# Half of the tokens of a product-key expert layer computed densely instead of gathered

## The chip, the cores and the metric

The program runs on one core of a Trainium2 chip. The metric is the device time of one execution in microseconds (us); the number given is the median of several runs. All data are f32.

## The reference, cut to what matters

Two transformer-like blocks follow each other on 512 tokens of width 1024. The change touches only the last part of the second block, a layer that picks 16 experts for each of 8 heads and each token, out of 128 x 128 = 16384 experts, each with one row u and one row v of 1024 numbers:

```python
q = (xb @ w_query).reshape(TOKEN_BLOCK, P_HEADS, 2, P_HALF)
s = jnp.einsum('thpk,hpnk->thpn', q, sub_keys)
sv, si = lax.top_k(s, P_TOPK)
cand = (sv[:, :, 0, :, None] + sv[:, :, 1, None, :]).reshape(TOKEN_BLOCK, P_HEADS, 256)
cidx = (si[:, :, 0, :, None] * N_KEYS + si[:, :, 1, None, :]).reshape(TOKEN_BLOCK, P_HEADS, 256)
fv, fpos = lax.top_k(cand, P_TOPK)
eidx = jnp.take_along_axis(cidx, fpos, axis=-1)
g = jax.nn.softmax(fv, axis=-1)
act = jax.nn.gelu(jnp.einsum('td,thkd->thk', xb, u_tab[eidx]))
out = jnp.einsum('thk,thkd->td', g * act, v_tab[eidx])
```

A residual sum and a final norm over each token follow.

## The kernel before

Each engine runs its own hand-written list of instructions, and semaphores order them. The 512 tokens are T = 4 tiles of 128, a token per partition in this stage. Weights stream through a ring of two 2 MB buffers (`ring`), loaded by the SP queue. The first layers take up to about 1355 us and stay as they are.

The expert stage begins with 32 projection chunks (`QUERIES`): each multiplies eight 128x128 weight tiles with 256 tokens (`chunk_pe`, L562), ScalarE copies the result (L1655), and `sub_scores` (L1416) multiplies it with the sub-keys. For each tile and head VectorE then runs a picking job in four pieces: `pick_keys` (top 16 of 128 scores, twice), `pick_pairs` (top 16 of the 256 sums), `pick_experts` (the expert numbers by comparing with `iota`), `pick_gates` (the softmax weights, with ScalarE's exponentials). There are 4 x 8 = 32 jobs.

A "pick" is one slot of one tile: NPICK = 512 of them, 128 per tile. For pick n GpSimd issues an indirect DMA (L2040) that fetches one row of `peer_uv` for each of the 128 tokens, u and v side by side, 8 KB per token, 1 MB in all, into a row buffer (`rows`, 10 to 14 slots in turn). VectorE makes the dot product with the token (`dot`, L1948), ScalarE the GELU and the weight (`weights`, L1630 and L1631), and then the row v is added with that weight, either on VectorE (`value`, L1960) or on TensorE: ScalarE writes a diagonal matrix of the weights (L1637), and TensorE multiplies it with v into two PSUM banks (`values`, L1468). `on_pe` sends about five of eight picks to TensorE. A row slot is free for the next gather when its value is done. VectorE runs picks in order, and puts one piece of a later job after every fourth pick; `lag_of` lets values trail the dot products by up to three picks. At the end of each tile five steps (`last`, L1969 to L1986) add the residual, norm and store.

## Time and profile before

| | us |
|---|---|
| median of 3 runs | 2700.69 |
| lowest, highest | 2699.71, 2701.6 |
| span of the profiled execution | 2699.1 |
| busy: TensorE (PE) | 2168.8 |
| busy: VectorE (DVE) | 1675.7 |
| busy: ScalarE (ACT) | 794.1 |
| busy: GpSimd (POOL) | 626.4 |

All profile numbers come from one execution. A view of groups gives, for a line of the program, an engine and an operation, the count, the busy time, the mean time of one in ns, and the idle time just before them with what ended it. A view of stretches gives the same busy times for a window of the span, with the clock that TensorE was granted (1.00 is 2.4 GHz) and the share of the 16 DMA engines that was busy. One f32 product of TensorE shows as two records, each with its own weight load (PEld); the 256 products of the query stage are 512 records. Durations of neighbouring records can overlap, so the distance of their starts is what a repeated operation costs.

### The profile page before, as it was taken

How to read it: one execution, taken by the hardware profiler on the slowest of the kernel's cores; microseconds unless marked ns; L12 is line 12 of the kernel's file. 1: busy time of each engine (PE TensorE's matmuls, PEld its weight loads, DVE VectorE, ACT ScalarE, POOL GpSimd, SP SyncE). 2: the span in 40 equal slices, each digit the busy share in tenths (PEclk: the TensorE clock that was granted, in tenths of full speed). 3: DMA queues.
4: the chain of work that ended last, by engine and by line, in shares of the span. 5: the costliest groups of instructions: out<-in, count | busy, mean ns of one | idle time of the engine just before them, and what ended most of it. 6: DMA issues, size and time to landing. Idle time of an engine off the chain costs nothing.

```text
span 2699.1 us, 20390 instructions
## 1 busy us (share of the span) xinstructions
PE 2168.8 (80%) x6274; PEld 1025.0 (38%) x6274; DVE 1675.7 (62%) x3651; ACT 794.1 (29%) x2184; POOL 626.4 (23%) x543
## 2 busy tenths in 40 slices
PE   6999999999999999999989666656565665556665
PEld 3454555444444444454478222223222222222221
DVE  5444454220114505234679888889889988889876
ACT  2022364110000002222333334334333334334332
POOL 0000000000000000000024444444444444444442
PEclk9999999999999999999999777888877788888778
DMA  9621010211236511211169999999999999999996
GB/s 371 241 102 63 32 63 32 80 76 62 89 129 258 210 62 65 76 47 63 47 236 370 407 427 427 427 427 427 427 427 427 427 426 425 428 425 420 421 423 275
DMA packets 85545, 692.66 MB, mean 257 GB/s; under 512 B 9504, under 2 KB 9504, under 8 KB 10688
## 3 DMA queue, kind: packets, MB, share of 16 engines
q0 software_dynamic: 77520, 590.33, 52.7%
q1 hardware_dynamic: 7200, 96.47, 9.4%
q10 hardware_dynamic: 720, 4.62, 0.4%
q8 instruction: 47, 0.77, 0.1%
q14 instruction: 58, 0.48, 0.0%
HBM read 689.28 MB, written 2.10 MB: 256 GB/s over the span
## 4 chain that ended last, share of the span: by engine, by line
PE 48%; DMA 29%; DVE 16%; issue 5%; POOL 1%; ACT 1%; POOLq 0%; DVEq 0%; ACTq 0%
PE PS L562 22%; DMA arena<-in_peer_uv,arena 20%; PE PS L592 8%; DMA ring<-in_peer_uv,arena 8%; DVE arena L1960 4%; PE PS L1104 4%; PE PS L1150 3%; DVE arena L1948 3%; PE PS L747 2%; PE PS L1468 2%; DVE ring L1948 1%; PE PS L767 1%; PE PS L756 1%; DMA arena<-in_ada 1%; PE PS L1125 1%
## 5 line engine op out<-in xcount | busy, mean ns | idle before, releaser
L1468 PE MATMUL PS<-arena 128*128 128x512 f32 x768 | 476.8, 771 | 320.1 <-ACT arena L1637 300.3
L2040 POOL DMA_INDIRECT arena<-in_peer_uv,arena x340 | 410.0, 1206 | 925.9 <-DVE arena L1930 461.5
L1948 DVE CUSTOM_DVE_ANT_0 arena<-arena 128x1024 f32<-128x1024 f32 x340 | 414.0, 1226 | 101.0 <-DMA arena<-in_peer_uv,arena 98.4
L1468 PEld LDWEIGHTS PS<-arena 128*128 128x128 f32 x768 | 177.1, 244 | 604.0 <-ACT arena L1637 415.7
L1468 PE MATMUL PS<-ring,arena 128*128 128x512 f32 x428 | 259.4, 755 | 138.9 <-ACT arena L1637 130.2
L562 PE MATMUL PS<-arena,ring 128*128 128x512 f32 x832 | 359.2, 593 | 2.1 <-issue 0.8
L1630 ACT ACTIVATE arena<-arena 128x1 f32<-128x1 f32 x512 | 103.2, 202 | 776.3 <-DVE arena L1948 775.5
L562 PE MATMUL PS<-hT,ring 128*128 128x256 f32 (+1 forms) x928 | 301.5, 486 | 7.0 <-ACT arena L1655 4.2
L2040 POOL DMA_INDIRECT ring<-in_peer_uv,arena x172 | 201.6, 1172 | 214.5 <-DVE arena L1960 159.4
L1948 DVE CUSTOM_DVE_ANT_0 ring<-ring,arena 128x1024 f32<-128x1024 f32 x172 | 209.1, 1226 | 45.2 <-DMA ring<-in_peer_uv,arena 42.8
L562 PEld LDWEIGHTS PS<-arena,ring 128*128 128x128 f32 x832 | 157.0, 190 | 203.2 <-issue 201.9
L562 PEld LDWEIGHTS PS<-hT,ring 128*128 128x128 f32 x928 | 179.9, 195 | 123.7 <-issue 99.9
L592 PE MATMUL PS<-hT,ring 128*128 128x512 f32 x512 | 222.1, 597 | 1.7 <-ACT hT L382 1.7
L2026 POOL DMA_DIRECT2D arena<-in_ada x20 | 10.7, 538 | 899.2 <-ACTq L343 668.5
L1468 PEld LDWEIGHTS PS<-ring,arena 128*128 128x128 f32 x428 | 101.0, 247 | 294.8 <-ACT arena L1637 183.2
L1960 DVE SCALAR_TENSOR_TENSOR arena<-arena 128x1024 f32<-128x1024 f32 x145 | 185.7, 1281 | 0.1
L1631 ACT ACTIVATE arena<-arena 128x1 f32<-128x1 f32 x512 | 150.8, 294 | 16.6
L592 PEld LDWEIGHTS PS<-hT,ring 128*128 128x128 f32 x512 | 98.0, 192 | 125.3 <-issue 124.2
L1780 DVE TENSOR_SCALAR arena<-PS 128x512 f32<-128x512 f32 x32 | 22.1, 691 | 196.0 <-PE PS L592 196.0
L1766 DVE SCALAR_TENSOR_TENSOR xT<-PS,modc,xT 128x512 f32<-128x512 f32 x24 | 18.0, 751 | 179.9 <-PE PS L562 179.9
L1637 ACT ACTIVATE arena<-cst,arena 128x128 f32<-128x128 f32 x299 | 120.1, 402 | 9.8
L1104 PE MATMUL PS<-hT,ring 128*128 128x512 f32 x256 | 117.9, 604 | 0.0
(321 smaller groups left out, 2231.4 us busy)
## 6 DMA issues: line engine op xcount, KB each, us to landing
ring<-in_wstream SPq DMA_DIRECT2D x45, 2048.0 KB, 7.5
arena<-in_ada POOLq DMA_DIRECT2D x24, 2048.0 KB, 8.7
arena<-in_peer_uv,arena POOLq DMA_INDIRECT x340, 17.6
ring<-in_peer_uv,arena POOLq DMA_INDIRECT x172, 17.6
xT<-in_xT POOLq DMA_DIRECT2D x1, 2048.0 KB, 18.5
arena<-in_alibi ACTq DMA_DIRECT2D x1, 2048.0 KB, 14.4
result<-arena SPq DMA_DIRECT2D x3, 512.0 KB, 7.7
arena<-in_subkeys ACTq DMA_DIRECT2D x1, 1024.0 KB, 4.8
```

The source lines that it names most:

```text
L562: ins = pe.matmul(o, l, r, start=(a == 0), stop=(a == len(lhs) - 1))
L592: ins = pe.matmul(bank(j % 2, n), w[:, k, m * P:(m + 1) * P], act_in(k), start=(k == 0), stop=(k == kc - 1))
L747: ins = pe.matmul(o, l, r, start=True, stop=True)
L1104: ins = pe.matmul(bank(7), w[:, k, tile(j % 4)], hT[:, k, :], start=(k == 0), stop=(k == KD - 1))
L1150: ins = pe.matmul(bank(5 + j % 2), lhs, rhs, start=(k == 0), stop=(k == KD - 1))
L1468: ins = pe.matmul(bank(6 + b), diag[:, k % NDIAG, :], rows[slot_of(n)][:, D + b * 512:D + (b + 1) * 512], start=opens, stop=closes)
L1630: own(act.activation(dots[:, e:e + 1], dots[:, e:e + 1], ACT.Gelu))
L1631: act.activation(wexp[:, t, e:e + 1], dots[:, e:e + 1], ACT.Copy, scale=gate[:, t, e:e + 1]).then_inc(wexp_ok, 1)
L1637: act.activation(diag[:, k % NDIAG, :], ident, ACT.Copy, scale=wexp[:, t, e:e + 1]).then_inc(diag_ok, 1)
L1948: dve.tensor_tensor_reduce(u, u, h2tok[t % 2], 1.0, 0.0, ALU.mult, ALU.add, dots[:, e:e + 1]).then_inc(dot_ok, 1)
L1960: dve.scalar_tensor_tensor(out=a, in0=v, scalar=wexp[:, t, e:e + 1], in1=a, op0=ALU.mult, op1=ALU.add)\
L2040: pool.indirect_dma_start(rows[j], None, ap["peer_uv"], bass.IndirectOffsetOnAxis(ap=eidx[:, t, e:e + 1], axis=0)).then_inc(landed[j], 16)
```

## The change

Tiles 0 and 1 (256 tokens) keep the gathers: NPICK is 256. For tiles 2 and 3 no row is gathered. Every expert is computed for all 256 tokens, and a table of gates, zero where an expert was not picked, selects:

- The experts are 128 chunks of 128; chunk j holds the experts i x 128 + j. `dense_dots(j)` multiplies u of the chunk (a new input `u_turned`, laid out for it, 0.5 MB per chunk) with the 256 tokens, eight products of 256 columns. `dense_gelu(m)` applies GELU to two chunks, `dense_weights(m)` multiplies them with the gates, and in the last loop TensorE multiplies the weights with v of the chunk (rows of `peer_uv` at a distance of 128 rows, 4 KB of each), four products of 512 columns, summed in PSUM over all chunks.
- The gate tables are a product of one-hot matrices: for each token, the first one-hots (128 picks x first key, times the gate) and the second ones (128 picks x second key). VectorE makes both: `first_one_hots` in 256 TENSOR_SCALARs of 128x128, `second_one_hots` in 32 TENSOR_TENSORs of 128x1024. TensorE multiplies them (`gate_tables`, 64 groups of four 128x128 products), ScalarE copies the result, and 16 blocks of 1 MB go to DRAM and are read back in another order, in pieces of 512 bytes, while the chunks run. A path that makes first one-hots on ScalarE exists in the code; `made_on_dve` returns True for all groups.
- The order: 24 "beats" first. Beats 0 to 15 hold one job of tile 2 or 3 and two picks each, beats 16 to 23 three picks; four beats also hold a job of tile 0. Beats 8 to 23 each make four groups of gate tables. The 56 picks of the beats have their values on TensorE, and dots and GELU of 24 chunks (AHEAD) run in beats 7 to 14. Queries alternate between the halves of the tokens, each pair of queries followed by its scores for two tiles, and ScalarE and TensorE put four queries to a beat.
- Then the last loop: TensorE runs chunks c = 0 to 127, each with the dots of chunk c + 24 and the values of chunk c. The 200 other picks run beside it, all with values on VectorE. `pick_at` ties a chunk to 1.73 picks.
- Row slots: 3 up to pick 13, 6 up to 35, then 7. The SP queue loads u (three buffers), v (three), and gates (two).
- The last steps of tiles 1, 2 and 3 follow each other after everything else.

```diff
+NGT = 2
+NPICK = NGT * NSLOT
 NDIAG = 4
+NCHUNK = 128
+AHEAD = 24
+NBEAT = 24
 BLK = 4096
...
+def made_on_dve(g):
+    return True
...
+def dense_pair(b, q):
+    m = 3 * (b - 7) // 2 + q
+    return m + 1 if 7 <= b < 15 and m < 3 * (b - 6) // 2 else 0
+def pick_at(chunk):
+    return NEARLY + (max(0, chunk) * 173) // 100
...
+            for j in range(AHEAD + 3):
+                if j == 0:
+                    sp.wait_ge(mm_done, MM0["pq"] + 1)
+                if j >= 3:
+                    sp.wait_ge(s_done, j - 2)
+                sp.dma_start(ubuf[j % 3], ap["u_turned"][j]).then_inc(u_loaded[j % 3], 16)
+            def load_values(j):
+                sp.dma_start(vbuf[j % 3], value_rows[j]).then_inc(vt_loaded[j % 3], 16)
+            def load_gates(blk):
+                sp.dma_start(gstage[blk % 2].rearrange("p (a c) -> p a c", a=16),
+                             gates_in_dram[:, :, blk * P:(blk + 1) * P].rearrange("a p c -> p a c")).then_inc(g_loaded[blk % 2], 16)
+            sp.wait_ge(g_pe, 64)
+            load_values(0)
+            for q in range(2):
+                sp.wait_ge(g_stored[q], 16 * 8)
+            load_gates(0)
+            load_values(1)
+            load_gates(1)
+            load_values(2)
+            for c in range(NCHUNK):
+                if c + AHEAD + 3 < NCHUNK:
+                    sp.wait_ge(s_done, c + AHEAD + 1)
+                    sp.dma_start(ubuf[c % 3], ap["u_turned"][c + AHEAD + 3]).then_inc(u_loaded[c % 3], 16)
+                if c + 3 < NCHUNK:
+                    sp.wait_ge(d_done, c + 1)
+                    load_values(c + 3)
+                if c % 8 == 0 and c // 8 + 2 < 16:
+                    sp.wait_ge(w_ok, 4 * (c // 8 + 1))
+                    load_gates(c // 8 + 2)
+                if c == 80:
+                    sp.wait_ge(fin_ok, 1)
+                    sp.dma_start(out[0:P, :], acc[0]).then_inc(stored, 16)
...
+            def dense_dots(j):
+                pe.wait_ge(u_loaded[j % 3], 16 * (j // 3 + 1))
+                if j % 2 == 0 and j >= 4:
+                    pe.wait_ge(s_ev, j // 2 - 1)
+                for k in range(KD):
+                    ins = pe.matmul(dense_bank(j), ubuf[j % 3][:, tile(k)], hT[:, k, 256:512], start=(k == 0), stop=(k == KD - 1))
+                ins.then_inc(s_done, 1)
+            def turn_picks(td):
+                pe.wait_ge(picks_ok, td + 1)
+                pe.wait_ge(pk_ev, 16)
+                if td == 1:
+                    pe.wait_ge(picks_ev, 1)
+                for q in range(2):
+                    pe.transpose(PS[:, 3, tile(q)], selij[:, td, q, :], ident)
+                pe.transpose(PS[:, 3, tile(2)], gate[:, 2 + td, :], ident).then_inc(picks_pe, 1)
+            def gate_tables(g):
+                if made_on_dve(g):
+                    pe.wait_ge(a_dve, MADE_DVE[g + 1])
+                else:
+                    pe.wait_ge(a_act, MADE_ACT[g + 1])
+                pe.wait_ge(b_ok, g // 2 + 1)
+                if g >= 2:
+                    pe.wait_ge(g_ev, g - 1)
+                for q in range(4):
+                    ins = pe.matmul(PS[:, 4 + g % 2, tile(q)], aone[:, g % 2, q, :], bone[:, (g // 2) % 2, 4 * (g % 2) + q, :],
+                                    start=True, stop=True)
+                ins.then_inc(g_pe, 1)
+            for b in range(6, NBEAT):
+                values(beat_picks(b - 1))
+                if b >= 7:
+                    for q in range(4):
+                        if q < 2 and dense_pair(b, q):
+                            dense_dots(2 * dense_pair(b, q) - 2)
+                            dense_dots(2 * dense_pair(b, q) - 1)
+                        if b in (8, 16) and q == 0:
+                            turn_picks(b // 8 - 1)
+                        if b >= 8:
+                            gate_tables(4 * (b - 8) + q)
+            values(beat_picks(NBEAT - 1))
+            pe.wait_ge(picks_ev, 2)
+            pe.wait_ge(g_ev, 64)
+            for c in range(NCHUNK):
+                if c + AHEAD < NCHUNK:
+                    dense_dots(c + AHEAD)
+                pe.wait_ge(w_ok, c // 2 + 1)
+                pe.wait_ge(vt_loaded[c % 3], 16 * (c // 3 + 1))
+                for td in range(2):
                     for half in range(2):
-                        ins = turn(hT, t + 1, half, half)
-                    ins.then_inc(tt_pe, 1)
-                    values(t * NSLOT + 36, t * NSLOT + 44)
-                    pe.wait_ge(tt_ev, 3 + t)
-                for half in range(2):
-                    ins = turn(xT, t, half, half)
-                ins.then_inc(x_turned, 1)
-                values(t * NSLOT + (44 if t + 1 < T else 36), t * NSLOT + 48)
-                if 0 < t < T - 1:
-                    scores_of(t + 1)
-                values(t * NSLOT + 48, n1)
+                        ins = pe.matmul(bank(2 + 2 * td + half), weights_of(c)[:, tile(td)], vbuf[c % 3][:, half * 512:half * 512 + 512],
+                                        start=(c == 0), stop=(c == NCHUNK - 1))
+                ins.then_inc(d_done, 1)
...
+            def dense_gelu(m):
+                act.wait_ge(s_done, 2 * m + 2)
+                if m == 8:
+                    act.wait_ge(pk_keys, JOB[2, PH - 1] + 1)
+                if 2 * m >= AHEAD:
+                    act.wait_ge(d_done, 2 * m + 2 - AHEAD)
+                act.activation(weight_pair(m), bank(m % 2).rearrange("p (c n) -> p c n", c=2), ACT.Gelu).then_inc(s_ev, 1)
...
+            def second_one_hots(m):
+                if m % 16 == 0:
+                    dve.wait_ge(picks_ev, m // 16 + 1)
+                if m >= 2:
+                    dve.wait_ge(g_pe, 2 * m - 2)
+                c = 8 * (m % 16)
+                dve.tensor_tensor(bone[:, m % 2, :, :], const("iota").unsqueeze(1).to_broadcast([P, 8, P]),
+                                  pick_j[:, c:c + 8].unsqueeze(2).to_broadcast([P, 8, P]), ALU.is_equal).then_inc(b_ok, 1)
+            def first_one_hots(g):
+                if g >= 2:
+                    dve.wait_ge(g_pe, g - 1)
+                for q in range(4):
+                    c = 4 * (g % 32) + q
+                    ins = dve.tensor_scalar(aone[:, g % 2, q, :], const("iota"), pick_i[:, c:c + 1], pick_g[:, c:c + 1],
+                                            ALU.is_equal, ALU.mult)
+                ins.then_inc(a_dve, 1)
+            def dense_weights(m):
+                blk = m // 4
+                dve.wait_ge(s_ev, m + 1)
+                dve.wait_ge(g_loaded[blk % 2], 16 * (blk // 2 + 1))
+                w = weight_pair(m).rearrange("p c (a t) -> p c a t", a=16)
+                g = gstage[blk % 2].rearrange("p (a c t) -> p c a t", a=16, t=16)[:, 2 * (m % 4):2 * (m % 4) + 2, :, :]
+                dve.tensor_tensor(w, w, g, ALU.mult).then_inc(w_ok, 1)
...
+            job(0)
+            gated = 0
+            for b in range(NBEAT):
+                if b < 16:
+                    k = JOB[2 + b // 8, b % 8]
+                    job(k, gated)
+                    gated = k
+                picks = beat_picks(b)
+                dot(picks[0])
+                if b in (16, 19, 23):
+                    pick_gates(gated)
+                for n in picks[1:]:
+                    dot(n)
+                if b in GATHER_JOB_AT:
+                    hd = GATHER_JOB_AT[b]
+                    k = JOB[hd // PH, hd % PH]
+                    if b < 16:
+                        job(k, gated)
+                    else:
+                        job(k)
+                    gated = k
+                if b >= 8:
+                    for q in range(4):
+                        g = 4 * (b - 8) + q
+                        if q % 2 == 0:
+                            second_one_hots(g // 2)
+                        if made_on_dve(g):
+                            first_one_hots(g)
+            done, m = NEARLY, 0
+            for n in range(NEARLY, NPICK):
                 dot(n)
                 while done < min(n + 1 - lag_of(n), NPICK):
-                    if not on_pe(done):
-                        value(done)
+                    value(done)
                     done += 1
-                if n in (1, 3, 5):
-                    pick(1, (n + 1) // 2)
-                if n % 4 == 1 and n // PK + 2 < NHEAD:
-                    pick(n // PK + 2, n % PK // 4)
-                t, e = n // NSLOT, n % NSLOT
-                if t > 0 and e in LAST_AT:
-                    last(t - 1, LAST_AT.index(e))
+                while m < NCHUNK // 2 and n >= max(NEARLY + 2 + m, pick_at(2 * m + 1 - 14)):
+                    dense_weights(m)
+                    m += 1
+                for back, piece in ((13, pick_keys), (11, pick_pairs), (9, pick_experts), (5, pick_gates)):
+                    hd = (n + back) // PK
+                    if (n + back) % PK == 0 and 5 <= hd < NGT * PH:
+                        piece(JOB[hd // PH, hd % PH])
+                if n >= NSLOT and n - NSLOT in LAST_AT:
+                    last(0, LAST_AT.index(n - NSLOT))
```

## Rows read from the trace of the kernel before

**Rows 1.** The page: busy tenths in 40 slices, granted clock, DMA share, GB/s.

```profile
PE   6999999999999999999989666656565665556665
...
DVE  5444454220114505234679888889889988889876
...
PEclk9999999999999999999999777888877788888778
DMA  9621010211236511211169999999999999999996
GB/s 371 241 102 63 32 63 32 80 76 62 89 129 258 210 62 65 76 47 63 47 236 370 407 427 427 427 427 427 427 427 427 427 426 425 428 425 420 421 423 275
```

**Rows 2.** Stretches: length, busy us of each engine (records), granted clock, DMA share, GB/s.

```profile
600.00:700.00 100.00, 100.00 (x234) 44.27 (x233) 9.67 (x14) 9.46 (x15) 0.00 (x0) 1.00 0.23 84
1000.00:1100.00 100.00, 97.07 (x281) 43.49 (x280) 38.33 (x62) 20.32 (x32) 0.00 (x0) 0.98 0.17 63
...
1450.00:1500.00 50.00, 42.54 (x207) 35.31 (x207) 47.58 (x89) 17.55 (x56) 24.68 (x18) 0.95 0.94 355
1500.00:1600.00 100.00, 64.19 (x116) 24.91 (x114) 87.76 (x187) 36.44 (x112) 49.04 (x42) 0.79 1.01 425
1600.00:1800.00 200.00, 121.14 (x200) 46.92 (x200) 176.13 (x378) 75.69 (x232) 94.87 (x81) 0.80 1.01 427
```

**Rows 3.** Timeline at the start of the query stage: start us, us, engine, line, operation.

```profile
1355.80 10.19 PE L562 MATMUL PS<-hT,ring 128*128 128x256 f32 x32 [1.72 <-ACT hT L382]
...
1366.56 0.68 PE L1416 MATMUL PS<-arena 128*128 128x128 f32 x4 [0.56 <-ACT arena L1655]
...
1367.69 0.49 DVE L1890 MAX8 arena<-arena 128x8 f32<-128x128 f32 x2 [8.18 <-ACT arena L1660]
...
1373.23 0.17 DVE L1920 TENSOR_SCALAR arena<-arena 128x16 uint32<-128x16 uint32 x1
1373.31 0.17 DVE L1921 TENSOR_SCALAR arena<-arena 128x16 uint32<-128x16 uint32 x1
...
1376.04 10.53 PE L562 MATMUL PS<-hT,ring 128*128 128x256 f32 x48
1376.19 0.17 DVE L1930 CAST arena<-arena 128x16 uint32<-128x16 f32 x1
...
1376.64 0.99 POOL L2040 DMA_INDIRECT arena<-in_peer_uv,arena  x1 [461.51 <-DVE arena L1930]
```

**Rows 4.** DMA queues from 1600 to 1800 us: packets, MB, share of 16 engines.

```profile
q0 software_dynamic: 11706, 85.28, 101.0%
```

**Rows 5.** DMA queues and issues in the last 9.1 us of the span.

```profile
q1 hardware_dynamic: 288, 0.52, 14.9%
...
result<-arena SPq DMA_DIRECT2D x2, 256.0 KB, 2.0
```

**Rows 6.** The gathers' line L2040: time from issue to landing.

```profile
DMA to landing us min/median/max: 5.6/17.6/23.1
```

**Rows 7.** Groups from 1340 us on, by form: busy, mean ns, idle before them.

```profile
L1948 DVE CUSTOM_DVE_ANT_0 arena<-arena 128x1024 f32<-128x1024 f32 x340 | 414.0, 1226 | 101.0 <-DMA arena<-in_peer_uv,arena 98.4 <-DVE arena L1902 0.4
...
L1960 DVE SCALAR_TENSOR_TENSOR arena<-arena 128x1024 f32<-128x1024 f32 x145 | 185.7, 1281 | 0.1
...
L1924 DVE TENSOR_TENSOR arena<-arena,cst 128x512 f32<-128x512 f32 x32 | 22.1, 692 | 1.1
...
L1972 DVE TENSOR_TENSOR arena<-arena,sq 128x1024 f32<-128x1024 f32 x4 | 4.9, 1219 | 0.0
```

**Rows 8.** Groups before 1350 us, by form: a TENSOR_SCALAR with two scalars.

```profile
L818 DVE TENSOR_SCALAR arena<-arena,smalls 128x128 f32<-128x128 f32 x16 | 5.5, 346 | 0.6
```

**Rows 9.** Timeline of the end: start us, us, engine, line, operation.

```profile
2685.79 1.23 DVE L1948 CUSTOM_DVE_ANT_0 arena<-arena 128x1024 f32<-128x1024 f32 x1 [1.21 <-DMA arena<-in_peer_uv,arena]
...
2689.64 1.22 DVE L1969 TENSOR_TENSOR arena<-arena,PS 128x1024 f32<-128x1024 f32 x1
...
2695.30 1.42 DVE L1986 SCALAR_TENSOR_TENSOR arena<-arena,smalls 128x512 f32<-128x512 f32 x2
```

614 lines of the change are left out of this document (371 added, 243 removed).

## The prediction

> **What bounds the kernel now.** I read the page's slices first [rows 1]. Up to about slice 20 TensorE is nine tenths busy at full clock; from there to the end the DMA engines are full, at 427 GB/s, and TensorE is down to five or six tenths at a granted clock of 0.7 to 0.8. So there are two stages with two limits. The table of stretches says the same with numbers [rows 2]: from 1500 us on TensorE is busy 64% or less and its clock is 0.79 to 0.80 of 2.4 GHz, the DMA share is 1.01, VectorE is busy 88%. The change touches only what follows 1356 us, where the last projection (the queries) starts [rows 3]; everything ahead of it is the same program.
>
> The tail is 512 gathers of 128 x 8 KB, 1.0486 MB each. At 427 GB/s one takes 2.456 us, and 512 take 1257 us. The first starts at 1376.6 [rows 3], the last dot product at 2685.8 [rows 9]: 1309 us. So 96% of that stretch is the gathers, and the row of the DMA engines shows that hardly anything else is moving [rows 4]. VectorE has 2.51 us of work on a pick that it handles wholly (1.226 + 1.281 us, [rows 7]), so it is close behind.
>
> **The change part by part.** It removes 256 gathers, half of the stage: 629 us of DMA time. In their place stand, for the other 256 tokens, all 128 blocks of 128 experts: the loads of u (128 x 0.524 MB in 4 KB rows), of v (as much), gate tables written once (16 x 1.049 MB) and read once (the same bytes in 512 B pieces), dense products on TensorE, and one-hot matrices that VectorE makes. By bytes that is 168 MB, 393 us at 427 GB/s. The DMA bill alone falls by 236 us. What spoils this is that the work now comes in two phases, one after the other: the beats (jobs, one-hots, gate tables) and the main loop (values).
>
> Terms that I use. A 512-column f32 product is two records of 0.427 us (234 records fill 100 us at clock 1.00, [rows 2]), so 0.854 us; a 256-column one is two of 0.219 us (48 in 10.53 us, [rows 3]), so 3.50 us for the 8 of a query or of a dense dot; four 128-column ones are 8 records, some 1.05 us (4 in 0.68 us, [rows 3]; down to 0.13 each). A picking job on VectorE, without waits, is 1367.69 to 1376.36 [rows 3], 8.7 us with its last conversion; with the gate step 9.1. A gather lands 5.6 us after its issue at the least [rows 6], and the issue takes about 1 us.
>
> *Queries and beats 0 to 7.* The first picking job now waits for a third query, 1372 in place of 1367.7. TensorE has 30 queries after the first two (105 us), 15 score groups (16 us), transposes (3), and values of 10 picks (17, each 1.71): from 1367 to 1508. Picks share three row slots in this part, so a slot passes from TensorE's value to the next gather, dot product and weight; that loop is about 19.6 us per beat, which is also what TensorE has to do in it. Picks 14 and 15 go to slots in the weight ring, which are free after the last query; with pick 13's slot freed at 1512 they land at 1519 or so. Job (2,7) follows: beat 8 starts at about 1532.
>
> *Beats 8 to 15.* VectorE has a job (9.1), two dot products (2.35) and four groups of one-hots. The first one-hots are 16 TENSOR_SCALARs of 128x128 with two operands of a scalar kind; the nearest row is 346 ns, and two in a row overlap by some 0.08 us, so 0.26 each [rows 8]. The bounds are 0.35 (no overlap) and 0.17 (half hidden, as with the 0.17 us steps of the first job that start 0.08 apart, [rows 3]); the second ones are two of 128x1024 at 1.22 [rows 7]. A group is 1.06 + 0.61. TensorE has 3.4 of values, 4.3 of gate tables and one or two dense pairs of 7.0. In the beats with two pairs (four of them) the second pair stands between two gate tables and VectorE must wait for it, because it has two buffers only: 23.9 us; in the others 18.2. With the extra job in beat 11 and the copying of the picks: 1532 + 17 + 96 + 64 + 13 = 1722 at the first table of beat 16.
>
> *Beats 16 to 23.* VectorE has 3.5 + 6.7 = 10.2 us per beat, TensorE 9.4, DMA 3 gathers and one table, 9.8: three about equal. Seven beats, two jobs (17.4) and the last groups: 94 us. The phase ends at about 1816, say 1810, as the dense jobs leave out two small steps. So 434 us pass from the first gather with only 213 us of DMA work in them. If the one-hots cost 0.17 us each this is 23 us shorter, at 0.35 it is 23 us longer.
>
> *Main loop.* It starts with a hole: the first gates must come back from DRAM, VectorE waits for them with the weights of pick 57 behind it, and ScalarE waits for two finished chunks at pick 57. 22 us pass before gathers run freely (7 picks are in slots by then). Then DMA has to do 193 gathers (474 us), 99 loads of u and 125 of v, 14 of gates, and 2.5 us of small ones. A 4 KB row: between a packet of 2 KB, 0.085 us (14.9% of 16 engines in 9.1 us is 21.7 us, for 256 of them, [rows 5]), and one of 8 KB in the full stretch (2.456 us for 8 per engine, 0.307); on that line it is 0.159, and 8 of them per engine are 1.27 us. u 126, v 159. A 512 B piece on the same line is 0.028 us, 128 per engine are 3.6 us, 14 loads 50 us; the low end is the bytes at 427 GB/s, 34 us, the high end a 2 KB packet's 0.085 us, 152 us. I take 50, the line's. Sum 812 us.
>
> TensorE in the same loop: 104 chunks of 3.50 + 3.42 and 24 of 3.42 are 802 us, at clock 1.00, from about 13 us after the start. That is the same as DMA, within 2%. VectorE: 200 picks of 2.51 (502), 11 jobs (100), 64 weight products of 0.69 (44), and 5: 651 us, not the bound. Two equal loads with buffers of three chunks lose a little to each other; I estimate 1%, 8 us, and count to 30 in the range.
>
> *End.* After the last row lands: dot 1.2, weight 1.5, two values 2.5, then twelve steps of the last three tiles at 1.22 (15, [rows 9] for the like), roots 1.5, store 2.5: 24 us, against 12 now.
>
> Sum: 1810 + 22 + 812 + 8 + 24 = 2676 us of span. The span now is 2699.1 and the median 2700.7, 1.6 more, so **2678 us**, 0.8% less. Nearly all of the 236 us of DMA time that is saved is given back while the DMA engines stand half idle in the beats.
>
> At one place a rule of the Trainium skill speaks against this. The rows of v for one chunk are i x 128 + j of a table of 8 KB rows: 4 KB pieces, 1 MiB apart from partition to partition. No row of this trace has such a pitch, the gathers being scattered and the weight blocks contiguous. "DMA: Bandwidth & Descriptors", section "Latency and other measured facts", gives copies at a pitch of 512 KiB 207 GB/s and at 2 MiB 164, where the full rate is 214. By the page the 159 us of v would be an estimate of 164 to 207.
>
> **Rivals.**
> *Slow pieces (slower).* The small or far-apart pieces of the gates and of v cost more than the line through 2 KB and 8 KB. Place: the main loop, DMA-bound. It decides from 17 us of extra on (2678 to 2695); a third more on v alone (53) gives 2731, all of the gates' high end (102) gives 2780. For it: none of these shapes is in the trace. Against: even the 2 KB packets run at 24 GB/s per engine, the same as large ones.
> *The clock (slower).* TensorE's clock was 1.00 and 0.98 at 100% and 97% busy, 0.95 at 85%, 0.79 at 64% [rows 2]. If waits for chunks keep it at a mean of 0.9 of 2.4 GHz, between these rows, its 802 become 891 us: 1810 + 13 + 891 + 17 + 1.6 = 2733. It decides below a mean of about 0.94. Against: a TensorE that is the bound is always busy, and then the clock comes back.
> *The beats are shorter (faster).* The one-hots are pipelined at 0.17 us and the pair between two tables costs VectorE nothing: 23 + 24 us off, and 2631. For it: small operations of the first job start 0.08 us apart. Against: the pair is TensorE's work in any case.
> That the change doesn't do what it says I leave out: half of the gathers go away whatever the rest does.
>
> **Chances.** Forecast 0.49 (2650 to 2706; six sevenths of it below 2695), shorter beats 0.16, slow pieces 0.22, the clock 0.13. A measurement of this kernel can tell 0.2% from no change, 5.4 us. Faster: 0.16 + 0.42 = 0.58; within 0.2% 0.07 (all of it from the forecast case); slower 0.35. The range is 2610 to 2765: it leaves out a tenth at each side.
>
> **What would show it.** Right: 256 gathers; DMA share near one half from 1380 to 1800 and near 1.0 afterwards; granted clock above 0.95 in the main loop; the last gate table's product at 1780 to 1840; TENSOR_SCALAR of 128x128 near 0.35 us with a start every 0.26. Wrong: a DMA share of 1.0 at much less than 427 GB/s in the main loop (slow pieces); TensorE always busy at a clock of 0.8 or 0.9; or VectorE or ScalarE waiting for each other in the main loop with both DMA and TensorE idle, which I hold at a few us only. The largest doubt is where the beats end; each us there is a us of the result.

## The result and the profile after

The changed kernel takes 2776.0 us (median of 4 runs, 2763.54 to 2777.31) against 2700.2 of the kernel before: ratio 1.0271, 95% interval 1.0250 to 1.0292. The prediction was 2678, 22 us faster; it came out 76 us slower, outside the range. The span of the profiled execution is 2775.0 us, the forecast of it was 2676.

The page after: slices for TensorE, granted clock, DMA and GB/s, then the two large queues (packets, MB, share of 16 engines).

```profile
PE   6999999999999999998998877668999999989877
...
PEclk9999999999999999999999999889999999999989
DMA  9621021112156411110244656779999999999995
GB/s 368 236 92 61 31 71 51 61 61 91 60 227 227 151 61 61 67 55 31 94 172 148 242 187 229 306 265 354 405 387 388 388 389 400 395 400 379 369 370 208
...
q0 software_dynamic: 40656, 321.93, 29.4%
q1 hardware_dynamic: 76944, 247.48, 24.4%
```

The shape is the forecast one: the DMA engines are half empty up to about slice 27 and full from slice 28 on. TensorE is nine tenths busy in most slices, with six to eight tenths in slices 22 to 28 (beats 8 to 23 and the start of the loop). What differs from [rows 1] is that the full DMA engines move 369 to 405 GB/s (slices 29 to 39) and not 427. By stretch (length, busy us of each engine, granted clock, DMA share, GB/s), with the main loop's 700 us as one:

```profile
1548.00:1725.00 177.00, 140.02 (x663) 111.59 (x664) 142.62 (x476) 77.37 (x130) 16.42 (x17) 0.92 0.57 202
1725.00:1830.00 105.00, 74.26 (x329) 50.32 (x328) 89.50 (x249) 54.77 (x104) 25.26 (x22) 0.85 0.71 276
...
1900.00:2600.00 700.00, 659.77 (x2224) 435.65 (x2223) 491.95 (x893) 124.80 (x407) 189.60 (x157) 0.96 0.99 387
```

The main loop is the counterpart of [rows 2]: both DMA (share 0.99) and TensorE (660 of 700 us) are nearly full, the clock is 0.96, and VectorE is idle for 30% of the time. It is idle because it waits, not because it has time to spare (below).

I split the 99 us between the forecast span and the real one at three marks. The last gate table's product starts at 1827.5 instead of 1810: 18. The first dense value starts at 1850.6, 23 us later; the hole of 22 is as forecast. The last dot product of a gather starts at 2725.8, so the loop took 876 us from 1850 where I had 812 + 8: 56. From there to the end are 49 us, not 24: 25. So: beats 18, loop 56, tail 25. The end of the kernel after, VectorE (start, us):

```profile
2725.82 1.22 DVE L2182 CUSTOM_DVE_ANT_0 arena<-arena 128x1024 f32<-128x1024 f32 x1
...
2761.40 1.22 DVE L2242 TENSOR_TENSOR arena<-PS,sq 128x1024 f32<-128x1024 f32 x1 [24.65 <-PE PS L1628]
```

In [rows 9] the last steps follow the last dot at once. Here VectorE waits 24.65 us for TensorE, which still has dense chunks to do.

What comes from memory in the main loop, by the page's DMA issues (count, KB each, us to landing): the gate tables, read in 512 B pieces, take 22.7 us to land, while 1 MB stored contiguously, when the DMA engines are half empty, takes 5.8.

```profile
arena<-in_u_turned SPq DMA_DIRECT2D x128, 512.0 KB, 9.0
arena<-in_peer_uv SPq DMA_DIRECT2D x128, 512.0 KB, 9.2
...
gate_tables<-arena ACTq DMA_DIRECT2D x16, 1024.0 KB, 5.8
arena<-gate_tables SPq DMA_DIRECT2D x16, 1024.0 KB, 22.7
```

### The profile page after: what moved, and what is told of

Same layout as the page of the kernel before. It is cut to its first block, busy times and chain, and to the rows that moved or that the text cites. A ratio compares the mean times of both kernels' runs of the same rounds, so it can differ in the third digit from the quotient of the medians.

```text
span 2775.0 us, 24927 instructions
## 1 busy us (share of the span) xinstructions
PE 2532.4 (91%) x8876; PEld 1459.4 (53%) x8876; DVE 1487.6 (54%) x3441; ACT 652.0 (23%) x1559; POOL 314.1 (11%) x287
## 4 chain that ended last, share of the span: by engine, by line
PE 73%; DMA 14%; DVE 10%; issue 1%; ACT 1%; SPq 1%; POOL 0%; DVEq 0%; ACTq 0%; POOLq 0%
PE PS L609 24%; PE PS L1579 12%; PE PS L1628 11%; DMA arena<-in_u_turned 9%; PE PS L639 8%; PE PS L1151 4%; PE PS L1197 3%; PE PS L794 2%; DMA arena<-in_peer_uv 1%; PE PS L1602 1%; PE PS L814 1%; PE PS L803 1%; DMA arena<-in_ada 1%; DVE arena L2221 1%; PE PS L1172 1%
## 5 line engine op out<-in xcount | busy, mean ns | idle before, releaser
L1579 PE MATMUL PS<-hT,arena 128*128 128x256 f32 x2048 | 488.4, 395 | 60.4 <-DMA arena<-in_u_turned 60.4
L1579 PEld LDWEIGHTS PS<-hT,arena 128*128 128x128 f32 x2048 | 406.5, 199 | 171.6 <-DMA arena<-in_u_turned 71.1
L609 PE MATMUL PS<-arena,ring 128*128 128x512 f32 x832 | 359.2, 593 | 2.1 <-issue 0.8
L2342 POOL DMA_INDIRECT arena<-in_peer_uv,arena x151 | 176.2, 1167 | 1158.3 <-DVE arena L2153 465.7
L2182 DVE CUSTOM_DVE_ANT_0 arena<-arena 128x1024 f32<-128x1024 f32 x151 | 183.9, 1222 | 97.5 <-DMA arena<-in_peer_uv,arena 95.5
L1628 PE MATMUL PS<-arena,hT 128*128 128x512 f32 x384 | 173.6, 598 | 14.1 <-DVE hT L2231 14.1
L1628 PE MATMUL PS<-arena,ring 128*128 128x512 f32 x320 | 146.6, 603 | 15.3 <-DMA arena<-in_peer_uv 15.2
L2182 DVE CUSTOM_DVE_ANT_0 ring<-ring,arena 128x1024 f32<-128x1024 f32 x105 | 127.9, 1223 | 38.8 <-DMA ring<-in_peer_uv,arena 37.3
L1628 PE MATMUL PS<-arena 128*128 128x512 f32 x320 | 143.9, 593 | 1.6 <-DMA arena<-in_peer_uv 1.4
L1602 PE MATMUL PS<-arena 128*128 128x128 f32 x512 | 78.7, 315 | 72.3 <-DVE arena L2221 68.9
L1602 PEld LDWEIGHTS PS<-arena 128*128 128x128 f32 x512 | 73.1, 223 | 83.8 <-DVE arena L2221 78.2
## 6 DMA issues: line engine op xcount, KB each, us to landing
arena<-gate_tables SPq DMA_DIRECT2D x16, 1024.0 KB, 22.7
```

The source lines that it names most:

```text
L609: ins = pe.matmul(o, l, r, start=(a == 0), stop=(a == len(lhs) - 1))
L1579: ins = pe.matmul(dense_bank(j), ubuf[j % 3][:, tile(k)], hT[:, k, 256:512], start=(k == 0), stop=(k == KD - 1))
L1602: ins = pe.matmul(PS[:, 4 + g % 2, tile(q)], aone[:, g % 2, q, :], bone[:, (g // 2) % 2, 4 * (g % 2) + q, :], start=True, stop=True)
L1628: ins = pe.matmul(bank(2 + 2 * td + half), weights_of(c)[:, tile(td)], vbuf[c % 3][:, half * 512:half * 512 + 512], start=(c == 0), stop=( ...
L2182: dve.tensor_tensor_reduce(u, u, h2tok[t], 1.0, 0.0, ALU.mult, ALU.add, dots[:, e:e + 1]).then_inc(dot_ok, 1)
L2342: pool.indirect_dma_start(rows[j], None, ap["peer_uv"], bass.IndirectOffsetOnAxis(ap=eidx[:, t, e:e + 1], axis=0)).then_inc(landed[j], 16)
```

## The experiments

Theories at the start. A: SyncE's queue is blocked while the gate load's 2048 pieces are taken in, so u and v come late and TensorE stalls. B: the 1 MiB pitch of v costs. C: the total of the gate loads on a full DMA is the price. D: the end of the beats passes on one to one. E came later: in the early beats VectorE's idle time is a wait inside a chain. The recorded expectations of single runs use some letters otherwise: their B is "only the packets' own time counts", and the D of gates_once is "only the held-up queue counts". The kernel before, taken again beside each group of runs, had medians of 2699.9 to 2701.7 us, so times of different groups can be compared.

**The queue after a gate load.** SyncE's queue in the kernel after (start, us, line):

```profile
2102.57 0.33 SPq L1313 DMA_DIRECT2D arena<-in_peer_uv  x1
2102.94 0.43 SPq L1316 DMA_DIRECT2D arena<-gate_tables  x1
2106.02 15.88 SPq L1330 DMA_DIRECT2D arena<-in_u_turned  x1
```

The load of u behind a gate load takes 15.88 us to issue instead of 0.33. TensorE, same stretch:

```profile
2119.60 3.60 PE L1628 MATMUL PS<-arena,ring 128*128 128x512 f32 x8
2128.47 6.67 PE L1579 MATMUL PS<-hT,arena 128*128 128x256 f32 x16 [5.27 <-DMA arena<-in_u_turned]
```

The dots come 5.27 us late and then run at half speed, 6.67 us instead of 3.62. TensorE had been idle before them, and the granted clock of their stretch is 0.54: nearly all of it at the lower level, 1.2 GHz. In the loop TensorE waits 12 times for u, 60.4 us in all. VectorE and GpSimd in the same stretch, then two rows by stretch (the last three numbers are granted clock, DMA share and GB/s):

```profile
2127.24 0.69 DVE L2231 TENSOR_TENSOR hT<-hT,arena 128x512 f32<-128x512 f32 x1 [10.16 <-DMA arena<-gate_tables]
...
2130.54 0.94 POOL L2342 DMA_INDIRECT arena<-in_peer_uv,arena  x1 [12.25 <-DVE arena L2199]
...
2128.50:2135.00 6.50, 6.50 (x17) 5.25 (x18) 6.29 (x16) 0.96 (x4) 0.94 (x1) 0.54 1.02 384
2135.00:2140.00 5.00, 5.00 (x17) 2.91 (x16) 4.86 (x11) 3.41 (x7) 2.61 (x2) 1.00 0.73 228
```

VectorE stands 10.16 us in front of `dense_weights`, which needs this gate load. The dots and values behind it in its list wait too, so no row slot comes free, and GpSimd issues no gather for 12.25 us. A little later the DMA engines run out of work: their share from 2135 to 2140 us is 0.73. Over the loop VectorE waits 154.2 us for gate tables, 14 times. The DMA queues in the 19 us behind the gate load, 2103 to 2122 (q0 the gathers, q1 SyncE's queue with gates, u and v):

```profile
q0 software_dynamic: 761, 5.46, 70.1%
q1 hardware_dynamic: 2107, 2.13, 34.1%
...
arena<-in_u_turned SPq DMA_DIRECT2D x1, 512.0 KB, 22.4
```

The engines are full. But SyncE's queue gets 34.1% of their time, where it has 41.2% on the loop's average (below), the gathers 70.1% where they have 57.5%, and u lands after 22.4 us instead of 9. So the gathers run ahead while what VectorE and TensorE wait for is held up. The Trainium skill's "DMA: Bandwidth & Descriptors", section "Queues, rings and completion order", says that each DMA engine takes turns between the queues, a packet at a time (a packet there is a group of descriptors). If so, a turn of SyncE's queue filled with 512 B pieces is a short one against a turn of 8 KB rows. These rows (34.1% against 70.1%) agree with that; no run isolates it.

### gates_whole: the gate tables read contiguously

```
-  sp.dma_start(gstage[blk % 2].rearrange("p (a c) -> p a c", a=16),
-               gates_in_dram[:, :, blk * P:(blk + 1) * P].rearrange("a p c -> p a c"))
+  sp.dma_start(gstage[blk % 2], gates_in_dram[blk])
```

> This kernel reads each 1 MB block of gate tables back as 128 rows of 8 KB in place of 2048 pieces of 512 bytes; the bytes are the same, but the gates are those of other experts, so its output is not the reference's. Theory A (the SP queue is held up: the load that follows a gate load takes 4 to 19 us to issue, so u arrives late and TensorE stops 2 to 12 us at each of the 14 blocks, some 70 us with the start): the long issues of the SP queue and TensorE's waits for u_turned (60 us) go away, and the time falls by 50 to 80 us, to 2695 to 2725. Theory B (the DMA engines are full and only packets count): 2048 packets of 0.0305 us become 128 of 0.33, 14 blocks x 1.3 us = 18 us less, about 2757.

The chunks get the gates of other experts in this run. Measured: 2716.36 us (2711.68 to 2725.08), ratio 1.0056 (1.0035 to 1.0076). 60 us go with the pieces, the bytes unchanged. (Its profiled execution is the slowest of the four; between the profiled spans it is 52 us.) Its SyncE queue and its main loop:

```profile
1979.62 0.43 SPq L1316 DMA_DIRECT2D arena<-gate_tables  x1
1982.70 0.33 SPq L1329 DMA_DIRECT2D arena<-in_u_turned  x1
```

```profile
1900.00:2600.00 700.00, 678.08 (x2335) 446.02 (x2334) 523.71 (x957) 130.47 (x430) 195.88 (x165) 0.99 1.01 411
```

No long issue, 411 GB/s, the clock 0.99. A gate load lands after 15.4 us instead of 22.7, and VectorE's waits for gate tables fall from 154.2 us to 78.5.

### gates_once: 14 of the 16 gate loads left out

The loads of the tables of blocks 2 to 15 are left out and `dense_weights` uses what is there.

> Leaves out the loads of gate blocks 2 to 15; the weights of all chunks are made with blocks 0 and 1, so the output is not the reference's. The loads took 14 x 128 pieces of 0.0305 us per engine, 55 us of DMA time in the loop. Theory C (the loop is DMA-bound throughout, and the 512 B pieces also hold u and v back behind them, since a piece gets its turn between 8 KB packets of the gathers): the 1 MB blocks as whole rows still cost 2.5 us each, so this is 35 us below the kernel that reads them whole (2716): 2675 to 2690. Theory D (only the held-up queue counts, and TensorE is the bound once it is gone): as with whole rows, 2705 to 2720.

Measured: 2680.7 us (2680.1 to 2683.62), ratio 0.9931 (0.9911 to 0.9950). The last dot moves from 2725.8 to 2636: 90 us of loop, for which my sum had 50. Its slices, its main loop, and the whole loop of this run and of the kernel after:

```profile
GB/s 375 237 109 64 32 64 32 72 86 63 75 140 255 219 63 63 63 63 63 46 112 149 221 190 196 249 305 258 416 417 416 416 414 415 404 412 417 415 403 219
```

```profile
1900.00:2600.00 700.00, 696.67 (x2390) 450.12 (x2388) 547.10 (x978) 134.84 (x451) 213.38 (x176) 1.00 1.01 413
...
1848.00:2636.00 788.00, 780.83 (x2638) 496.27 (x2639) 607.45 (x1068) 145.87 (x496) 232.22 (x193) 1.00 1.00 407
...
1850.00:2726.00 876.00, 798.16 (x2622) 513.07 (x2623) 606.51 (x1068) 149.81 (x496) 232.53 (x193) 0.95 0.98 381
```

Against gates_whole that is 36 us for 14 contiguous loads, 2.5 us each, their bytes at full rate and no more. So pieces of 512 B cost 60 us more than the same bytes in long ones. Their own packets explain only a part: a piece has a mean duration of 0.0305 us in the trace's packet records, 128 per engine and load are 3.9 us, 14 loads 55; the whole ones 35. That is 20 of the 60. The other 40 are in what shares the engines and the buffers with them.

The packet records divide the loop itself. From the first dense value to the last dot it takes 875 us in the kernel after and 788 in gates_once. The packets' own times in it, summed and divided by 16 engines, are 857 and 790 (records of neighbouring packets overlap a little, so full engines come out at slightly more than the time). Of the 88 us, 54 are the pieces themselves. 13 are other packets that take longer beside them: 8 KB ones 0.324 us instead of 0.318, 4 KB ones 0.166 instead of 0.163. The remaining 21 are time in which the engines had too little to do. In gates_once VectorE waits for no gate table in the loop, and TensorE hardly for u. So neither A nor C alone explains the loads: most of the price is on the full DMA engines (C), the rest in engines that wait (A, and VectorE, which A didn't name).

The second fact of this run: even without the pieces the full rate is at most 417 GB/s, not the 427 of [rows 1].

### gates_in_four: the same pieces in four loads

Each gate load in four parts of 512 pieces, behind four successive chunks.

> Each gate block is loaded in four parts of 512 pieces, one after the v load of each of the chunks 8k to 8k+3, instead of all behind chunk 8k. Pieces and bytes are unchanged. Theory A (SP queue held up by one long transfer): no issue is held for more than about 5 us, which the three buffers of u and v cover; TensorE's waits for u fall from 60 us to under 15, and the time to 2705 to 2735. Theory B (the DMA engines are full): no change, 2770 to 2780.

Measured: 2784.47 us (2776.56 to 2789.49), ratio 1.0320 (1.0299 to 1.0341). No gain, and outside what both theories expected; issues of 2 to 12 us still stand behind many of the parts, and TensorE waits 61.4 us for u, where theory A expected under 15. So the long issues are not a matter of one long load. But the edit does a second thing: the last part of a gate load leaves three chunks later, and VectorE's waits for gate tables grow from 154.2 to 202.4 us. The run doesn't separate the two.

### v_whole: v read contiguously

```
-  sp.dma_start(vbuf[j % 3], value_rows[j])
+  sp.dma_start(vbuf[j % 3], ap["u_turned"][j])
```

> The v loads read the contiguous u blocks in place of rows 1 MiB apart, so its output is not the reference's. The rival of slow far-apart rows: packets of 4 KB (0.171 us on average, 0.159 in the median) fall to 0.159 and the time by 10 to 20 us or more. Theory A: the pitch costs nothing, 2770 to 2780, as TensorE's waits are for u and not for v.

Measured: 2774.56 us (2768.82 to 2778.38), ratio 1.0277 (1.0252 to 1.0302), the same as the kernel after. A 4 KB packet has a mean of 0.166 us in the loop, here as in the kernel after. Theory B falls: the pitch costs nothing.

### stored_in_pieces: the pieces moved to the stores

Loads as in gates_whole; the transposition of blocks is made by the stores, in the beats, where the DMA engines have time. The whole result is computed.

```
-  act.dma_start(gates_in_dram[tg], gstage[tg % 2])
+  act.dma_start(gates_in_dram[:, :, tg * P:(tg + 1) * P].rearrange("k p c -> p k c"),
+                gstage[tg % 2].rearrange("p (k c) -> p k c", k=16))
```

> The 512 B pieces move from the loads of the last loop to the 16 stores in beats 8 to 23, where the DMA engines are 30 to 40% idle; the result stays complete. Theory C: the last loop is that of the whole rows (2716), and the stores, 10 us or more apart, hide their pieces; the first gate load lands earlier too, so the start hole of 23 us shrinks by up to 10: 2705 to 2720. If stores in pieces are slow (over 10 us each) and ScalarE waits for the buffer, the beats get longer: 2725 to 2760.

Measured: 2723.76 us (2718.77 to 2726.67), ratio 1.0086 (1.0063 to 1.0109). 52 us back, 4 short of the expected range; the last product of a gate table starts about a us later (1828.7), and ScalarE waits 9.4 us for stores.

### half_values: is TensorE the bound of the loop?

Half of the dense value products (one of the two tiles of dense tokens) are left out, 218 us of TensorE.

> Leaves out half of the dense value products (those of the fourth tile), 256 products of 512 columns, 218 us of TensorE's 802 us in the last loop; all loads, gates and picks stay. Theory C (the loop is bound by the DMA engines): the last dot product stays near 2726 and only the end shortens, by about half of TensorE's 36 us behind it: 2750 to 2765. The rival that TensorE is the bound: 100 to 200 us less. With less to do TensorE's clock may fall; that changes nothing for C.

Measured: 2750.39 us (2748.45 to 2754.3), ratio 1.0194 (1.0176 to 1.0213). Of 218 us, 26 come back: the last dot is at 2714.8, 11 earlier, and the tail 34 us in place of 49. TensorE's granted clock in this loop is 0.88, lower than the 0.95 of the kernel after, and the loop is still shorter. So TensorE doesn't bind the loop. By these rows the DMA engines (share 0.99) do, with VectorE's waits for gate tables, 159 us here, beside them; the time in which the DMA engines had too little to do falls from 18 us to 8.

### slope160 and stored_slope: the tail

The planner's spread of chunks over picks at 1.60 instead of 1.73; stored_slope has it on top of stored_in_pieces.

> One number: the last loop ties a chunk to 1.60 picks in place of 1.73. Theory (the end): the picks end 48 us before the kernel does, because TensorE has some 13 chunks of 3.4 us left by then; ScalarE lets picks run ahead to the edge that pick_at sets. With 1.60 TensorE is 7 chunks further at the same pick, so the tail shrinks by about 20 us. As the DMA time is unchanged, the last dot product comes some 5 us later: 2755 to 2765. If the tail is not set by this edge, no change.

> Both edits: stores in pieces, and 1.60 picks per chunk. If the two are independent, 2716 less 15 to 20: about 2697, the time of the kernel before.

Measured: slope160 2756.75 us (2755.23 to 2759.57), ratio 1.0207 (1.0187 to 1.0226); the last dot is 7.5 us later (2733.3), the wait for TensorE is gone and the tail is 24. stored_slope 2721.78 us (2718.51 to 2723.45), ratio 1.0075 (1.0055 to 1.0095): only 2 us better than stored_in_pieces, since the last dot goes from 2678.6 to 2697. I had added the two gains; with TensorE 697 of 700 us busy and DMA at 1.01 in the loop of stored_slope (1900 to 2600), the work that leaves the tail has no room ahead of it.

### half_on_act and pair_last: the length of the beats

half_on_act makes every second group of first one-hots on ScalarE. pair_last puts the second dense pair of a beat behind the fourth gate table, on TensorE and on ScalarE.

> Every second group of first one-hots is made on ScalarE (eight ACTIVATEs of 128x128, some 0.4 us each, 3.2 us per group) in place of VectorE (1.1 us per group). If VectorE is the bound of beats 8 to 23, at most 32 x 1.1 = 35 us go and the last gate table comes at about 1800 in place of 1828. If ScalarE, which also copies a gate table in 1.05 us and has the weights of the picks, becomes late in its place (2 x 3.2 + 4 x 1.05 + 3 = 14 us per beat against 10 to 11 now), the beats 16 to 23 get longer by 3 us each and the time rises by about 10 to 30 us. I hold the second for likelier: 2785 to 2805.

> In beats 8, 10, 12 and 14 the second dense pair comes behind the fourth gate table instead of between the first and the second. My sum had 23.9 us for such a beat against 18.2, because VectorE waits for the pair. If that wait is the price, the last gate table comes 9 us (TensorE's own 21.7 us per beat then bound) to 23 us earlier than 1828, and the time falls by as much, to 2752 to 2766. If VectorE's 28 us of waits were covered otherwise, no change.

Measured: half_on_act 2835.27 us (2831.47 to 2837.97), ratio 1.0497 (1.0476 to 1.0519), 30 us above the expected range: the last gate table moves by 58.7 us and the time by 59. pair_last 2759.29 us (2752.95 to 2765.0), ratio 1.0232 (1.0212 to 1.0252): table 18 and time 17 us earlier; VectorE's waits for TensorE fall from 28.4 to 12.2 us. Theory D holds in both directions. Those waits in the kernel after (VectorE; the first two are in beats with two pairs, the last two are gathers that had not landed, in beats with three picks):

```profile
1560.39 1.12 DVE L2221 TENSOR_SCALAR arena<-cst 128x128 f32<-128x128 f32 x4 [8.42 <-PE PS L1602]
...
1601.49 1.11 DVE L2221 TENSOR_SCALAR arena<-cst 128x128 f32<-128x128 f32 x4 [5.86 <-PE PS L1602]
...
1742.29 1.23 DVE L2182 CUSTOM_DVE_ANT_0 ring<-ring,arena 128x1024 f32<-128x1024 f32 x1 [4.51 <-DMA ring<-in_peer_uv,arena]
...
1799.23 1.23 DVE L2182 CUSTOM_DVE_ANT_0 arena<-arena 128x1024 f32<-128x1024 f32 x1 [4.22 <-DMA arena<-in_peer_uv,arena]
```

### stored_pair and stored_pair_three: a version that uses this

stored_pair is stored_in_pieces with pair_last. stored_pair_three also takes three picks in beats 8 to 15, with the spread at 1.64.

> Stores in pieces (2724) and the pair behind the tables. If each us of the beats is a us of the result: 2700 to 2715.

> As before, with three picks instead of two in beats 8 to 15 (64 picks in the beats in place of 56, the fourth job of tile 0 moved from beat 18 to 15) and 1.64 picks per chunk. 8 picks less in the DMA-bound loop are 8 x 2.6 = 21 us less there; each costs the beats 1.2 us of VectorE or 1.7 of TensorE, 10 to 14 us. So 7 to 11 us below the kernel without it, 2690 to 2708. If the beats can't take the picks, no gain.

Measured: stored_pair 2713.41 us (2705.64 to 2719.33), ratio 1.0055 (1.0038 to 1.0073); stored_pair_three 2701.89 us (2691.28 to 2708.48, 10 runs), ratio 1.0009 (0.9994 to 1.0024). That is the kernel before.

### jobs_early and all_early: the gather jobs in beats 1 to 4

VectorE seems idle half the time in the early beats, so the four gather jobs go there.

```
-GATHER_JOB_AT = {4: 1, 11: 2, 18: 3, 22: 4}
+GATHER_JOB_AT = {1: 1, 2: 2, 3: 3, 4: 4}
```

> The four jobs of tile 0 stand in beats 1 to 4 (now 4, 11, 18, 22), where VectorE waits for row slots and queries: it is busy 85 of 153 us up to 1508. Theory (a us of the beats is a us of the result, and VectorE sets the beats from 8 on): three jobs of 8.7 to 9.1 us leave the bound part, the last gate table comes 20 to 27 us before 1828 and the time falls by as much, 2748 to 2756. Rival: the beats 16 to 23 are held by the gathers or TensorE just behind VectorE, then under 10 us: 2765 or more.

> The kernel with stores in pieces, the pair behind the tables and three picks per beat (2702), with the same four jobs in beats 1 to 4. By the same theory two jobs leave beats 11 and 15 and one beat 22, 17 to 26 us: 2676 to 2685, below the kernel before by 0.6 to 0.9%. By the rival, above 2692.

Measured: jobs_early 2765.34 us (2762.74 to 2778.0), ratio 1.0234 (1.0219 to 1.0250); all_early (on stored_pair_three) 2714.14 us (2706.9 to 2715.28), ratio 1.0040 (1.0026 to 1.0054). Both missed. The gate-table beats became 27 us shorter (from first to last table 251 instead of 279), as counted, but the beats before them 23 us longer. VectorE, jobs_early:

```profile
1425.48 1.23 DVE L2182 CUSTOM_DVE_ANT_0 arena<-arena 128x1024 f32<-128x1024 f32 x1 [14.34 <-DMA arena<-in_peer_uv,arena]
1451.61 1.22 DVE L2182 CUSTOM_DVE_ANT_0 arena<-arena 128x1024 f32<-128x1024 f32 x1 [5.73 <-DMA arena<-in_peer_uv,arena]
1477.39 1.22 DVE L2182 CUSTOM_DVE_ANT_0 arena<-arena 128x1024 f32<-128x1024 f32 x1 [5.37 <-DMA arena<-in_peer_uv,arena]
```

and the kernel after:

```profile
1424.87 1.23 DVE L2182 CUSTOM_DVE_ANT_0 arena<-arena 128x1024 f32<-128x1024 f32 x1 [14.21 <-DMA arena<-in_peer_uv,arena]
1444.02 1.23 DVE L2182 CUSTOM_DVE_ANT_0 arena<-arena 128x1024 f32<-128x1024 f32 x1 [7.89 <-DMA arena<-in_peer_uv,arena]
1462.93 1.22 DVE L2182 CUSTOM_DVE_ANT_0 arena<-arena 128x1024 f32<-128x1024 f32 x1 [7.65 <-DMA arena<-in_peer_uv,arena]
```

The beats are 26 us apart instead of 19, and the wait for the second row of a beat is still 5.4 to 5.7 us. An engine that waits inside a chain (value, gather, landing, dot, weight, and the value again) is not free: work behind the last dot delays the next beat's start.

### jobs_in_wait, all_in_wait and pair_in_wait: the jobs in the wait itself

The same four jobs, but each between the first and the second dot of its beat, where VectorE waits for the landing.

```
                 dot(picks[0])
+                if b in GATHER_JOB_AT:
+                    hd = GATHER_JOB_AT[b]
+                    k = JOB[hd // PH, hd % PH]
+                    job(k, gated)
+                    gated = k
                 for n in picks[1:]:
                     dot(n)
```

> The kernel after with the four gather jobs of the beats in beats 1 to 4 (as in jobs_early), but each put between the first and the second gather's dot of its beat, where VectorE waits 7.7 to 14 us for the second row to land, instead of behind both. Theory E (beats 1 to 4 are a chain value, gather, landing, dot, weight; work put into its wait is free, work put behind it lengthens it): the wait of 5.4 to 7.7 us goes and each of the four beats is about 20.5 us instead of 26 in jobs_early (19 in the kernel after), the first gate table is copied at about 1555 (jobs_early 1571.5, after 1548.7), the last near 1806 (1822.7, 1827.5); time about 2750 to 2757. Rival (the dot of the second row is what the chain needs next, so anything ahead of it lengthens the beat as much as behind it): first gate table at 1568 or later, the last near 1820, time 2763 or more.

> all_early (whole gate loads with the 512 B pieces on the store side, second dense pair after the fourth gate table, three picks in beats 8 to 15, gather jobs in beats 1 to 4) with the gather jobs put between the two dots in the same way. Theory E: first gate table near 1555 (all_early 1568.2), last near 1830 (1845.4), time 14 to 18 us under all_early, about 2696 to 2702, which only equals the kernel before. Rival: 2710 or more, as all_early.

Measured: jobs_in_wait 2745.4 us (2739.2 to 2748.2, 5 runs), ratio 1.0163 (1.0149 to 1.0178). all_in_wait 2693.19 us (2687.8 to 2702.97, 11 runs), ratio 0.9973 (0.9963 to 0.9984): 7 to 8 us under the kernel before, three tenths of a percent, and less than expected by 3 us or more. The gate-table products of jobs_in_wait (count, min/median/max ns, first to last start):

```profile
L1602 PE MATMUL PS<-arena x512: 272/275/582, 1544.8 to 1796.2; 128*128 128x128 f32 x171
```

against those of the kernel after:

```profile
L1602 PE MATMUL PS<-arena x512: 272/275/583, 1548.7 to 1827.5; 128*128 128x128 f32 x171
```

31 us earlier at the end, 31 us less time. Theory E holds, and better than I had priced it: the first table isn't late at all, and the time is 5 us under the expected range. all_in_wait gained 9 us over stored_pair_three where jobs_in_wait gained 31 over the kernel after. To see what stands in its place I took three picks back to two:

> The kernel after with the 512 B pieces on the store side, the second dense pair after the fourth gate table, the gather jobs of beats 1 to 4 between the two dots (as in jobs_in_wait), two picks in every beat to 15 as in the kernel after, and the spread of the chunks at 1.68 picks each in place of 1.73. It differs from all_in_wait by two picks instead of three in beats 8 to 15, so 8 more of the gathers are done in the last loop. Theory E with the DMA-bound loop: the last gate table is copied at about 1785 to 1790 (stored_pair 1809.7, less what jobs_in_wait gained less what pair_last already had), the last loop is about 12 us longer than that of all_in_wait, time about 2685 to 2697. Rival (ScalarE's wait for the stores in pieces, 37 us in all_in_wait, sets the pace of the beats once VectorE doesn't): last gate table at 1800 or later and time about 2700 or more.

Measured: 2703.03 us (2693.64 to 2708.01, 11 runs), ratio 1.0001 (0.9991 to 1.0011); the last table's product is at 1813.2, where stored_pair had 1814.2. The rival named in the expectation came true. ScalarE's copies of the gate tables in that run (busy, mean ns, idle before and what ended it):

```profile
L1835 ACT ACTIVATE arena<-PS 128x512 f32<-128x512 f32 x64 | 64.6, 1048 | 66.4 <-DMA gate_tables<-arena 38.6 <-PE PS L1601 26.2 <-ACT arena L1835 1.5
```

ScalarE waits 38.6 us for the stores in pieces, with two staging buffers (18.4 us in stored_pair). With contiguous stores and the same jobs in the wait, jobs_in_wait has its last table at 1796.2. So once VectorE's jobs are out of the way, these stores most likely set the pace of the beats. A third staging buffer, which would show it, was not tried.

## Why the prediction was wrong, by its own steps

Three steps failed. In the main loop (56 us) the gate loads were priced at their own packets alone, with nothing for what they do to other packets and to VectorE and TensorE, which wait for loads. At the end (25 us) the dense chunks left after the last pick had no term. In beats 16 to 23 (18 us) VectorE's waits for gathers had none.

*Queries and beats 0 to 7:* right. The first product of beat 8 is at 1548.7, the forecast 1532 + 17 = 1549.

*One-hots:* right. Eight TENSOR_SCALARs of 128x128 take 2.13 or 2.14 us in the timeline of the kernel after, 0.27 each, forecast 0.26 from [rows 8]. The group's mean is 345 ns, [rows 8] has 346.

```profile
1730.17 2.13 DVE L2221 TENSOR_SCALAR arena<-cst 128x128 f32<-128x128 f32 x8
```

*Beats 8 to 15:* right. The first product of beat 16, behind the transposes of its picks (L1589), is at 1721.1, the forecast 1722:

```profile
1717.33 0.38 PE L1589 MATMUL PS<-cst,arena 128*128 128x128 f32 x2
...
1721.07 5.83 PE L1602 MATMUL PS<-arena 128*128 128x128 f32 x32 [3.25 <-DVE arena L2221]
```

VectorE's waits for TensorE are 28.4 us, nearly all of them here, where I had 4 x 5.7 = 23 for the second dense pairs. What made up for the 5 isn't assigned.

*Beats 16 to 23:* all of the 18 us, which pass one to one into the time (half_on_act, pair_last, jobs_in_wait). From 1721.1 to 1827.5 are 106 us for the forecast 94. I called VectorE, TensorE and DMA equal there and added nothing for what equal loads lose to each other. VectorE waits three times for a gather, 3.2 to 4.5 us each, 12 together, as much as the difference. The other 6 are those that I took off (1816, "say 1810") without a price; they didn't come.

*Main loop, gates:* the step that failed most. The price of a piece was nearly right, 0.0305 us for 0.028 (the line between 2 KB and 8 KB gives 0.0295, so the 50 should have been 53). But I added the pieces' own packet time, as if other packets and the engines that wait were indifferent to them. I had 651 us of work for VectorE, called it "not the bound", and gave no price to its wait for a table. gates_once shows 90 us of loop for these loads, gates_whole that 60 of the total are due to the pieces. By the packet records 54 are the pieces, 13 are slower neighbours, and in 21 the DMA engines had too little to do. For these 21 the trace shows two waits: VectorE's for the gate tables, 154.2 us (78.5 with whole rows), behind which no gather is issued, and TensorE's for u, 60.4 us (L1579; 26.8 with whole rows). half_values gives 10 of the 21 back by taking work from TensorE; how they divide between the two waits otherwise stays open. Dividing the load in four didn't help, but it made VectorE wait longer, so it doesn't settle which of them counts. A third gate buffer, with which a gate load could leave earlier, was not tried. Of my rivals it was slow pieces: the place was right, but the pieces themselves ran at the line's price, and what they cost beyond it was the waits and the neighbours. The size is about 40 + 16, below its 102 of the high end.

*Main loop, u, v and gathers:* the rest of the 56 is 16. Without gate loads the forecast was 820 - 50 = 770 us, and gates_once took 786 (1850 to 2636). The full rate with 4 KB and 8 KB packets mixed is at most 417 GB/s, where gathers alone have 427 [rows 1]: 770 x 427/417 = 788 (796 with 413, the mean from 1900 to 2600). By queues: gathers had 101.0% x 16 x 200 us for 85.28 MB of 8 KB packets [rows 4], 0.310 us each, and have 57.5% x 16 x 700 for 162.18 MB, 0.325, in the kernel after:

```profile
q0 software_dynamic: 22260, 162.18, 57.5%
q1 hardware_dynamic: 49218, 108.08, 41.2%
```

My line between a 2 KB and an 8 KB packet gave 0.159 for 4 KB, against 0.166. It is a small error per packet, on a full resource.

*The pitch of v:* the price of 159 held but for the 0.166 above. The Trainium skill's "DMA: Bandwidth & Descriptors", section "Latency and other measured facts", has a loss for copies between HBM tensors at power-of-two pitches of 512 KiB and more (207 GB/s at 512 KiB and 164 at 2 MiB, for 214). No such loss shows for this load of 4 KB rows at 1 MiB: v_whole, without the pitch, is within 0.1% of the kernel after.

*Two equal loads:* 8 us of interference was not far off for the two of them without gate loads (786 measured for 788). What I left out is that TensorE has nothing to catch up with: after a stall it is behind for good, and the planner's 1.73 picks per chunk left work for the tail. That reading fits half_values and slope160, which both shorten the tail; no run isolates a single stall.

*Tail:* 24 was the price of VectorE's steps and is right (slope160: 24). The other 25 us are dense chunks after the last pick, which I had put inside the loop. With another spread they go, the last dot comes 7.5 us later, and the time falls by 19.

*The clock:* 0.95 over the loop (1850 to 2726), 1.00 in gates_once where the stalls are gone. Its rival needed a mean of 0.94 or less and TensorE as the bound. It was near, and dots behind a stall do run at half speed. But half_values has 0.88 and a shorter loop, so the clock wasn't what set the time.

*Shorter beats:* no. The pair between two tables does cost VectorE its wait, and the one-hots are not at 0.17.

The sum, mended: 1828 + 22 + (770 + 16 + 90) + 49 = 2775, with about 35 of the 90 not in the pieces themselves.

## What to carry to other kernels

When two resources are both to be full, a sum of each one's own work is a lower bound: small pieces on a full DMA cost what they hold up besides their own time (here about 35 us of loop on top of 55), so put them where the engines are idle, even if that is the other end of the same transfer. An engine can be idle a third of the time and still hold up the rest, when what it waits for stands in front of other work in its list. Work moved into an engine's idle time is free only inside the wait, not behind it: the same four jobs changed the time by -11 us behind the last dot of a beat and by -31 us ahead of it. A phase that only feeds the next one passes its length on one to one, so price it like the loop itself.
